# Longer halved tails ahead of the norms, two units in the first paced loop behind them, and four weight remainders per norm formed by GpSimd

## The reference, cut to what matters

```python
y = rms_norm(r, g)                  # or layer_norm(r, g, b): r @ statistics over the 1024 features
h = silu(y @ w_gate) * (y @ w_up)   # or the first products of a mixer
r = alpha * r_or_y + h @ w_down     # r_or_y: r in the first block, y in the second; then the next norm
```

## Time and profile before

| | |
|---|---|
| median of three runs | 4340.07 us (4335.52 to 4343.68) |
| the profiled execution | 4341.47 us |
| its span, first to last instruction | 4339.6 us |
| TensorE matmuls busy | 3873.5 us (89%) |
| VectorE, ScalarE, GpSimd busy | 2154.8 us (50%), 1239.4 us (29%), 210.6 us (5%) |
| mean granted TensorE clock | 0.907 |
| chain that ended last | TensorE 72%, VectorE 16%, ScalarE 3% |

### The profile page before, as it was taken

The page is one execution under the profiler, slowest core; times in us unless marked ns, Lnnn a source line. Parts: engine busy times, 40 slices in busy tenths (PEclk is TensorE's granted clock), DMA queues, the critical chain, the costliest instruction groups (busy, mean ns, idle before and its releaser), DMA issues.

```text
span 4339.6 us, 43087 instructions
## 1 busy us (share of the span) xinstructions
PE 3873.5 (89%) x17308; PEld 2994.1 (69%) x17308; DVE 2154.8 (50%) x3241; ACT 1239.4 (29%) x2115; POOL 210.6 (5%) x399
## 2 busy tenths in 40 slices
PE   7988998999885559999999897699999999999997
PEld 5645745888751138888888764488888888568886
DVE  7444624643568866434443725364345435336434
ACT  3231222322231113223322322032223224433222
POOL 0000000000057600000000000000000000000000
PEclk9868967999976669999999988599999999999999
DMA  2201200223210002232323220022322232002221
GB/s 101 69 1 60 83 0 25 93 97 102 89 52 0 0 15 88 97 101 80 112 97 107 70 68 0 3 77 97 100 94 90 96 105 85 15 20 78 97 98 68
DMA packets 88634, 296.42 MB, mean 68 GB/s; under 512 B 15534, under 2 KB 16948, under 8 KB 88436
## 3 DMA queue, kind: packets, MB, share of 16 engines
q1 hardware_dynamic: 79844, 289.56, 19.9%
q10 hardware_dynamic: 8592, 4.12, 0.4%
HBM read 291.54 MB, written 2.10 MB: 68 GB/s over the span
## 4 chain that ended last, share of the span: by engine, by line
PE 72%; DVE 16%; ACT 3%; issue 1%; DMA 0%; ACTq 0%; DVEq 0%
PE ps L304 20%; PE ps L305 20%; PE ps L306 20%; PE ps L301 13%; DVE XT L632 1%; DVE WL L292 1%; DVE RS L677 1%; DVE VA L675 1%; DVE VA L676 1%; DVE od_w L1763 1%; DVE XT L634 1%; DVE od_w L1764 1%; ACT XH L503 0%; ACT wa_pt L2002 0%; ACT R L501 0%
## 5 line engine op out<-in xcount | busy, mean ns | idle before, releaser
L304 PE MATMUL ps<-XH,WH 128*128 128x512 f32 (+1 forms) x3376 | 1258.4, 373 | 85.5 <-DVE XL L640 52.4
L305 PE MATMUL ps<-XL,WH 128*128 128x512 f32 (+1 forms) x3376 | 1242.8, 368 | 0.0
L306 PE MATMUL ps<-XH,WL 128*128 128x512 f32 (+1 forms) x3376 | 1241.9, 368 | 0.0
L292 DVE TENSOR_TENSOR WL<-RAW,WH 128x1024 fp32r<-128x1024 f32 x548 | 665.0, 1230 | 315.5 <-ACT WH L286 309.2
L304 PEld LDWEIGHTS ps<-XH,WH 128*128 128x128 f32 x3376 | 653.5, 194 | 202.7 <-issue 53.3
L305 PEld LDWEIGHTS ps<-XL,WH 128*128 128x128 f32 x3376 | 654.0, 194 | 102.3 <-issue 3.4
L306 PEld LDWEIGHTS ps<-XH,WL 128*128 128x128 f32 x3376 | 653.2, 193 | 100.8
L286 ACT ACTIVATE WH<-RAW 128x1024 fp32r<-128x1024 f32 x548 | 565.4, 1048 | 127.1 <-PE ps L301 81.0
L304 PE MATMUL ps<-HH,WH 128*128 128x512 f32 (+1 forms) x1188 | 435.2, 366 | 0.0
L305 PE MATMUL ps<-HL,WH 128*128 128x512 f32 (+1 forms) x1188 | 434.1, 365 | 0.0
L306 PE MATMUL ps<-HH,WL 128*128 128x512 f32 (+1 forms) x1188 | 434.1, 365 | 0.0
(11 more groups left out here) (555 smaller groups left out, 3780.4 us busy)
## 6 DMA issues: line engine op xcount, KB each, us to landing
RAW<-units SPq DMA_DIRECT2D x548, 512.0 KB, 3.3
XIN<-in_x ACTq DMA_DIRECT2D x2, 1024.0 KB, 6.4
out<-OUT SPq DMA_DIRECT2D x4, 512.0 KB, 2.7
da_pi<-in_positions ACTq DMA_DIRECT2D x1, 256.0 KB, 3.9
od_pi<-in_positions ACTq DMA_DIRECT2D x1, 256.0 KB
wa_dist<-constants ACTq DMA_DIRECT2D x1, 192.0 KB, 2.3
da_lb<-in_ev_lambdas ACTq DMA_DIRECT2D x1, 128.0 KB, 3.6
od_bin<-in_od_b_re ACTq DMA_DIRECT2D x1, 128.0 KB
```

The lines of the kernel that those rows point to most:

```text
L292: nc.vector.tensor_tensor(WL[:, u % RING, :], RAW[:, u % RING, :], WH[:, u % RING, :].bitcast(F32), ALU.subtract)\
L304: nc.tensor.matmul(out, wh, xh, start=start, stop=False)
L305: nc.tensor.matmul(out, wh, xl, start=False, stop=False)
L306: return nc.tensor.matmul(out, wl, xh, start=False, stop=stop)
```

## The change

- `TAIL`: the last two tiles of a SwiGLU and the last four of a mixer are computed in halves, for one and three. In a SwiGLU `stats_pe(.., 0)` stands behind the first unit of tile (6, 1).
- Finishing: behind t = 2 VectorE finishes all half-1 tiles of the tail but the last, and the last one behind t = 7, ahead of `chain(e, 1)`. ScalarE's squares follow this (the last one behind its t = 7).
- `first_units`: TensorE runs over k with units 0 and 1 only, then does `stats_pe(.., 1)`, and then half 0 of units 2 and 3.
- Splitting: behind a SwiGLU nothing of the next stage is split ahead of the norm; units 0 and 1 are split behind t = 3 and t = 5 (`HI_AT`). Behind a mixer units 0 and 1 are split ahead of the norm. ScalarE copies units 2 and 3 behind t = 7, 4 and 5 behind t = 10 and 13.
- GpSimd forms the remainders of units 2 to 5 behind each norm but the last (`lo_behind`). `lo_to` skips them, and VectorE waits for GpSimd's last one before its next remainder.
- The sums of a half share bank 5, and `OUT_BANK` is reordered to suit.

```diff
-        TAIL = dict(load=8, ffn=1, ev_attn=0, ev_mamba=3, od=3, win=3, mlstm=3)
+        TAIL = dict(load=8, ffn=2, ev_attn=0, ev_mamba=4, od=4, win=4, mlstm=4)
...
+        pool_units = [e["n1"] + u for e in plan if e["kind"] == "norm" and not e["final"] for u in range(2, 6)]
...
         def lo_to(dve, n):
             for u in range(split["lo"], min(n, n_units)):
+                if u in pool_units:
+                    split["lo"] = u + 1
+                    continue
+                if u - 1 in pool_units:
+                    dve.wait_ge(S["split_ready"], u)
...
-            for u in range(3):
+            for u in range(2):
                 pe.wait_ge(S["split_ready"], n0 + u + 1)
             for k in range(KD):
                 pe.wait_ge(S["x_ready"], x0 + k + 1)
-                for u in range(3):
+                for u in range(2):
                     half(u, k, HALVES[0])
-                if k == 4:
-                    stats_pe(pe, nrm, 1)
-            pe.wait_ge(S["split_ready"], n0 + 4)
-            for k in range(KD):
-                half(3, k, HALVES[0])
+            stats_pe(pe, nrm, 1)
+            for u in range(2, 4):
+                pe.wait_ge(S["split_ready"], n0 + u + 1)
+                for k in range(KD):
+                    half(u, k, HALVES[0])
...
-            for m in range(KD - 1):
+            for m in range(KD - 2):
...
-            pe.wait_ge(S["r_ready"], e["r0"] + KD - 2)
-            down(KD - 1, ps[:, 7, HALVES[0]], HALVES[0], False).then_inc(S["tail_done"], 1)
-            pe.wait_ge(S["r_ready"], e["r0"] + KD - 1)
-            down(KD - 1, ps[:, 6, HALVES[1]], HALVES[1], True, lambda: stats_pe(pe, e["norm"], 0))
+            for q in range(KD - 2, KD + 2):
+                m, h = e["tiles"][q]
+                pe.wait_ge(S["r_ready"], e["r0"] + q - 1)
+                last = down(m, ps[:, 6 + m % 2, HALVES[h]], HALVES[h], h == 1,
+                            (lambda: stats_pe(pe, e["norm"], 0)) if q == KD else None)
+                if h == 0:
+                    last.then_inc(S["tail_done"], 1)
...
-                hi_to(act, min(n + 3, n - 3 * KD + 3 * q + 8 if e["kind"] == "ffn" else n - KD + q + 5))
-            hi_to(act, n + 3)
+                if e["kind"] == "ffn":
+                    hi_to(act, min(n, n - 3 * KD + 3 * q + 8))
+                else:
+                    hi_to(act, min(n + 2, n - KD + q + 5))
...
+            def lo_behind(e):
+                for u in range(e["n1"] + 2, e["n1"] + 6):
+                    if u == e["n1"] + 2:
+                        pool.wait_ge(S["split_ready"], u)
+                    pool.wait_ge(S["wh_ready"], u + 1)
+                    nc.gpsimd.tensor_tensor(WL[:, u % RING, :], RAW[:, u % RING, :], WH[:, u % RING, :].bitcast(F32), ALU.subtract)\
+                        .then_inc(S["split_ready"], 1)
...
                     if t == 2:
-                        second.get(e["prod"]["kind"], mixer_tail(1))(e["prod"])
-                    if t == 5:
-                        lo_to(dve, nx + 4)
+                        rest(prod, KD, KD + prod["tail"] - 1)
+                    if t == 7:
+                        rest(prod, KD + prod["tail"] - 1, KD + prod["tail"])
+                    if t in HI_AT:
+                        lo_to(dve, nx + HI_AT[t])
                     if t == 7:
                         chain(e, 1)
                         normed(8)
-                    if t in (10, 13):
-                        lo_to(dve, nx + {10: 5, 13: 6}[t])
...
-OUT_BANK = (4, 5, 0, 1, 2, 6, 7, 3)
+OUT_BANK = (5, 0, 1, 2, 4, 6, 7, 3)
+HI_AT = {3: 1, 5: 2, 7: 4, 10: 5, 13: 6}
```

More of the change, by code:

```diff
@@ L421, in _ @@
             nc.gpsimd.memset(ones[:], 1.0).then_inc(S["const_ready"], 1)
+            def lo_behind(e):
[5 more added lines that the diff above has]
+                        .then_inc(S["split_ready"], 1)
             for e in plan:
+                if e["kind"] == "norm" and not e["final"]:
+                    lo_behind(e)
                 if "pool" in mixers.get(e["kind"], {}):
@@ L504, in norm @@
                     if t == 3:
-                        for q in range(KD, KD + prod["tail"]):
+                        for q in range(KD, KD + prod["tail"] - 1):
                             square_act(act, prod, q)
[L507 to L510, removed]
+                    if t == 7:
+                        square_act(act, prod, KD + prod["tail"] - 1)
+                        if final:
+                            outs(0, 4)
+                    if t in HI_AT:
+                        hi_to(act, nx + HI_AT[t])
             def outs(a, z):
@@ L552, in finish, with ffn_tail @@
                     own(v.tensor_tensor(S2[:, hs], SQ[:, 0, hs] if m == 1 else S2[:, hs], SQ[:, m % 2, hs], ALU.add), "s2_added")
-            def ffn_tail(h):
-                def go(e):
+            def ffn_tail(e, a, z):
+                for q in range(a, z):
+                    m, h = e["tiles"][q]
                     if h:
-                        dve.wait_ge(S["unit_done"], e["n1"])
+                        dve.wait_ge(S["unit_done"], e["n1"] - 3 * (KD - 1 - m))
                     else:
-                        dve.wait_ge(S["tail_done"], e["t0"] + 1)
-                    finish(e, KD - 1 + h, ps[:, 7 - h, HALVES[h]], e["alpha"])
-                return go
@@ L563, in mixer_tail @@
[L563 to L576, removed]
-                        dve.wait_ge(S["xt_ready"], q + 1)
-                        finish(e, q, ps[:, 6 + q % 2, 0:HT], None)
-                return go
@@ L581, in _, with mixer_tail @@
-            second = dict(load=load_half(1), ffn=ffn_tail(1))
+                        dve.wait_ge(S["tail_done"], e["t0"] + m - KD + 3)
+                    finish(e, q, ps[:, 6 + m % 2, HALVES[h]], e["alpha"])
+                    if q == KD - 2:
+                        lo_to(dve, e["n1"])
+            def mixer_tail(e, a, z):
+                for q in range(a, z):
+                    m, h = e["tiles"][q]
+                    if h:
+                        dve.wait_ge(S["unit_done"], e["n1"] - (KD - 1 - m))
+                    else:
+                        dve.wait_ge(S["tail_done"], e["t0"] + m - KD + 5)
+                    finish(e, q, ps[:, OUT_BANK[m], HALVES[h]], e["alpha"])
@@ L583, in load, with load_tiles @@
+            def load_tiles(e, a, z):
+                for q in range(a, z):
+                    dve.wait_ge(S["xt_ready"], q + 1)
+                    finish(e, q, ps[:, 6 + q % 2, 0:HT], None)
+            second = dict(load=load_tiles, ffn=ffn_tail)
             def load(e):
-                load_half(0)(e)
+                load_tiles(e, 0, KD)
                 dve.wait_ge(S["vec_ready"], 1)
@@ L624, in norm @@
             def norm(e):
-                ln, final, nx = e["ln"], e["final"], e["next"]
+                ln, final, nx, prod = e["ln"], e["final"], e["next"], e["prod"]
+                rest = second.get(prod["kind"], mixer_tail)
                 def normed(t):
@@ L658, in norm @@
                         normed(8)
-                    if t in (10, 13):
-                        lo_to(dve, nx + {10: 5, 13: 6}[t])
             stages = dict(load=load, ffn=ffn, norm=norm,
-                          **{k: (lambda m: lambda e: m["dve"](dve, own, e, finish, mixer_tail(0)))(m) for k, m in mixers.items()})
+                          **{k: (lambda m: lambda e: m["dve"](dve, own, e, finish, mixer_tail))(m) for k, m in mixers.items()})
             for e in plan:
```

28 lines of the change are left out of this document (14 added, 14 removed).

## The result

The changed kernel takes **4365.49 us** (median of four runs, 4363.29 to 4372.49), the kernel before beside it 4337.94 (four runs). The ratio is 1.0064, with a 95% interval of 1.0048 to 1.0079: 27.6 us slower. The forecast was 4358. The profiled execution took 4366.26 us, its span 4364.4.

What follows compares the result with a forecast made beforehand. Each norm's seam was taken to be bound by VectorE's sum, covered by TensorE's work or not. The terms, 3 x 3.0 + 2 x 2.0 + 2.4 + 3.5 + 2 x 0.6 + 1.5 - 3.5 = +18 us, gave 4358 us; range 4335 to 4380.

Steps and rivals of the forecast that it cites:

- Steps 1 and 2: Norm behind SwiGLU with LayerNorm: first chain 7.1 us earlier; TensorE's cover grows from 5.0 to 13.0 us, ending its 4.32 us wait.
- Step 3: Same norm: TensorE, dry at +12.8, waits 6.8 us for the first two units' remainders, until +19.6 after the first chain's start.
- rival D: The wait for the first units' remainders is absent because ScalarE and VectorE run ahead: -2.5 at five norms, 4346 us.
- Step 4: Same norm: half 1's sums wait behind the two-unit loop over k; second chain at +29.5 instead of +20.6, 1.8 us later by clock.
- Step 5: Second half of that norm: GpSimd's subtractions hold VectorE, +0.6 us each, 1.2 for two; last x 3.0 us later per norm.
- Rival A: Second half's tiles at t = 10 and 13: GpSimd's subtractions don't hold VectorE; -8 us, 4332 us; chance 0.12.
- B: The two cancel: no lower clock in the loop over k, or GpSimd needs 1.9 us; +5 to +8, 4346 us; chance 0.20.
- The price of the subtraction: One GpSimd remainder subtraction, taken as 2.13 us from a listed two-tile subtraction or addition; bounds 1.89 and 3.14 us.
- rival C: Second half: GpSimd at 2.4 us or late semaphores idle TensorE into the lower clock, 2 to 3 us at five norms; 4376; 0.16.
- RMS behind a mixer ... +0.6 each: Two norms: the product's second half is bound by TensorE, which hides most of the delay; +0.6 us each.
- RMS behind a SwiGLU: Two norms, TensorE waiting some 2.5 us: +2.4 us into a SwiGLU, +3.5 into the S5/MLA mixer, where all of it shows.
- The last norm: No product or GpSimd work behind it; second chain at +19.7 instead of +15.2: -2.7, or -4.6 if clock holds; taken -3.5 us.

Runs made afterwards that it cites:

- e3: The changed kernel with units 0 and 1 behind a SwiGLU split behind t = 0 and 1 instead of 3 and 5: 4361.15 us.
- e5: The changed kernel with VectorE forming all remainders and, behind a SwiGLU, units 0 and 1 split behind t = 0 and 1: 4334.98 us.
- e1: The changed kernel with all 40 remainders back on VectorE, none by GpSimd: 4357.14 us.
- e2: The kernel before with its own tails, GpSimd forming only the remainders of units 3 to 5 behind each norm: 4353.28 us.
- e10: e1 plus four short GpSimd subtractions, reading two SBUF tiles and needed by nobody, beside each of units 2 to 5: 4411.34 us.
- e6: The changed kernel with GpSimd forming the remainders of units 2 and 3 only, VectorE those of 4 and 5: 4356.10 us.
- e11: e1 plus four GpSimd memsets, which read nothing and which nobody needs, beside each of units 2 to 5: 4349.77 us.
- the repetition: The changed kernel, unchanged, profiled a second time: 4366.22 us.
- e8: Against the kernel before: no GpSimd, mixers as before; behind a SwiGLU halved tails, early remainders, last tile finished behind t = 4, sums at k = 5: 4329.83 us.
- e12: e1 plus eight GpSimd memsets instead of e11's four beside each of units 2 to 5: 4354.48 us.

## Why the prediction was right

The sign, the range and the mechanism held; the size was 27.6 where I had 18 (24.8 by the spans). Part of that is luck: I put the untouched stages at nothing, and one of them costs other kernels of this set up to 11.5 us, which here would have meant some 4375.

- **Steps 1 and 2** held: in every SwiGLU stage the changed kernel takes 7.0 us less from the end of one seam to the first chain of the next, 7.1 forecast, and the old wait at +9.2 is gone.
- **Step 3**, the gate, held to 0.2 us: 6.95 ended by a WL of line 292 (now 298), forecast 6.8 and +19.6. e3 and e5 show that it was worth 10 to 11.3 us over five seams. The wait of 6.95 is itself against rival D.
- **Step 4** held: second chain at +29.7, forecast +29.5 (its terms add to 29.3). Behind a mixer with LayerNorm it came at +25.4; the terms there add to +25.3, not to the +25.1 in the text.
- **Step 5**, the hold on VectorE, held in kind: each subtraction that met a tile held it for 2.1 us (2.5 listed for 0.42), 1.4 at one seam, where its own remainder took 1.23 and a wait of 0.34. Of the 40 subtractions 28 held one row each; 12 met no row that waits. One of the signs that I named is missing: line 632 (now 652) has no long row, because it had always begun before the subtraction. Rival A falls with the held rows (e1, e2, e10), and B with the sum. A's own price was wrong besides: by my bound of -3.0 a seam behind a SwiGLU would be 1.2 us earlier, not 1.5 later.
- **The price of the subtraction** was mis-sized: I took 2.13 from the addition; its 40 rows took 2.34 to 2.65 us, median 2.40. The estimate of 2.3 by the Trainium skill (GPSIMD Engine Reference, "Elementwise — side-by-side cycle accounting") was nearer than my row. Of rival C the price came true and the threshold did not: at this seam TensorE's second-half wait is 3.58 us and the granted clock behind it 0.50, but they are 3.51 and 0.50 in e1 without GpSimd. So this low clock is no cost of the change. The kernel before has both too, which I had overlooked:

```profile
3265.26 0.58 PE L304 MATMUL ps<-XH,WH 128*128 128x256 f32 x1 [4.73 <-DVE XL L640]
```

- **"RMS behind a mixer ... +0.6 each", the step that failed.** Measured 3.3 and 2.0. I argued that the second half is bound by TensorE and hides VectorE's delay. At the first of the two it does hide what falls between the tiles (0.0; at the second 1.5 shows), but the first pair falls on the second chain and on TensorE's wait for unit 2, ahead of that half, and costs 3.1 and 1.6. "GpSimd's first two fall into VectorE's idle time" is true of a LayerNorm seam behind a SwiGLU, where VectorE waits 6.69 us, and I let it stand for seams where the second chain comes 18 us after the first. The first norm took 3.4 for 1.5: e6 gives the first pair 1.5 and the second 1.7 there, but this seam moves by 1.3 to 1.6 in e5 and e11 too, so the cause isn't shown.
- **LayerNorm**: 3.5, 3.3 and 3.3 us behind a SwiGLU for 3.0, and 2.9 and 2.8 behind a mixer for 2.0, in the direction of the dearer subtraction. **RMS behind a SwiGLU**: 2.4 for 2.4, and 4.3 (2.9 in the repetition) for 3.5 into the S5/MLA mixer; the prediction shows the working of neither, only the gate's wait of some 2.5 us (measured 3.1 and 2.7). Whether "all of it shows" holds stays open: TensorE's wait for that mixer's loads was 9.80 and 9.12 us in the two traces of the kernel before, 8.91 and 9.26 in those of the changed one.
- **The last norm** gave 2.6, as its sum at the lower clock said (2.7); taking 3.5 between that and 4.6 was the error.

The terms sum to 31.2 - 2.6 = 28.6 for 18; the untouched stages gave 3.8 back in this execution and 1.2 in the repetition.

## What to carry to other kernels

Before work goes from VectorE to GpSimd, ask what it reads: here the change bought 1.5 us of VectorE per remainder and paid 2.1 in waiting, wherever VectorE was needed. Place the moved instruction at every seam by that seam's own times; idle time found at one kind of seam is not there at another. When a longer cover is bought ahead of a wait, look at what else has to be ready at its end: the longer tails cost nothing any more once the remainders of the first units were formed early (e5), and paid in e8. That run changed several things at once; against e5 its seams and last norm gained 6.9 us, 3.3 of them at the last norm, where the last tile is finished earlier, 1.9 at the five seams behind a SwiGLU and 1.7 at the others. Which of its edits gives which part was not taken apart.

## What the runs showed of the hardware that I had not expected

- **Which VectorE rows wait.** Beside GpSimd's subtraction the chain's rows that read the sums in PSUM kept their 0.42 us (all 9 in the changed kernel); rows with two SBUF inputs that began beside it took 1.9 to 2.5. But the int32 rows of lines 692 and 693 have one SBUF input, and they took 0.82 to 2.37 for 0.29. I had looked for two inputs only. Those rows were the only ones that GpSimd's memsets lengthened at all, to 0.37 and 0.52 at most (e12). The Trainium skill (SBUF — State Buffer, "Who interferes with whom") has both: two SBUF inputs contend with a GpSimd instruction that reads and not with one that only writes, and `tensor_scalar` can run in a mode that takes GpSimd's ports whatever it does. The traces agree with the first. They fit the second, but no run shows which mode those rows ran in.
- **Each GpSimd instruction held one VectorE row, and who began first went on.** Behind a held row the next one runs at once: in e10 four GpSimd reads lengthened four VectorE rows to 0.83 to 0.96, and the fifth was at 0.43 again. The other way round a VectorE remainder that began 0.04 us earlier made the first of those reads 1.78 us long instead of 0.72. Sixteen such reads per seam cost 5.6 us, with VectorE's own work unchanged; the change's four long ones cost 2.4 after the four remainders that VectorE no longer forms.
- **An untouched stage took up to 11.5 us more at the lower TensorE clock in some kernels**, alike in both traces where a kernel was traced twice. Such a loss is almost half of this change's effect, and it is why e1's whole time alone would have put GpSimd's share at a third of what the seams show.
